# Loading and multiplying the first weight chunks of a decoder layer by rows of blocks

## The reference, cut to what matters

```python
def rms_norm(x, g):
    y = xf * lax.rsqrt(jnp.mean(xf * xf, axis=-1, keepdims=True) + EPS)
    return (y * g.astype(jnp.float32)).astype(x.dtype)

def swiglu(h, w_gate, w_up, w_down):
    return (jax.nn.silu(h @ w_gate) * (h @ w_up)) @ w_down

h = rms_norm(x, ffn1_norm[i])
x = x + 0.5 * swiglu(h, ffn1_w_gate[i], ffn1_w_up[i], ffn1_w_down[i])
```

## Time and profile before

| what | value |
|---|---|
| median of 3 runs | 938.45 us (937.75 to 938.58) |
| profiled execution, its own time | 938.35 us |
| its span, first to last instruction | 936.6 us |
| PE busy | 923.4 us, 99% of the span |
| ACT, POOL, DVE busy | 385.3, 414.0, 297.9 us |

### The profile page before, as it was taken

How to read it: one execution, slowest core, us unless ns; L and a number is a source line. 1 busy time by engine, 2 the same in 40 slices (tenths; PEclk the granted TensorE clock), 3 DMA queues, 4 the chain that set the end, 5 groups by cost and what they waited for, 6 DMA issues and landing times.

```text
span 936.6 us, 11393 instructions
## 1 busy us (share of the span) xinstructions
PE 923.4 (99%) x4104; PEld 759.6 (81%) x4104; DVE 297.9 (32%) x467; ACT 385.3 (41%) x514; POOL 414.0 (44%) x191
## 2 busy tenths in 40 slices
PE   7999999999999999999999999999999999999998
PEld 5888888888888888777788788888888888888886
DVE  6511122211100501659978532111112200410532
ACT  5734444433321421565844644433444321321641
POOL 3554444444444444345645354444444444444340
PEclk9999999999999999999999999999999999999999
DMA  8333333332332333231223143333333323332221
GB/s 251 108 113 99 102 90 94 108 90 90 107 95 90 90 112 90 60 99 34 68 68 113 54 126 103 99 90 94 107 90 91 108 93 90 99 103 90 74 73 56
DMA packets 129650, 89.25 MB, mean 95 GB/s; under 512 B 11312, under 2 KB 114776, under 8 KB 129624
## 3 DMA queue, kind: packets, MB, share of 16 engines
q1 hardware_dynamic: 129608, 88.90, 31.9%
q10 hardware_dynamic: 16, 0.00, 0.0%
HBM read 86.80 MB, written 2.10 MB: 95 GB/s over the span
## 4 chain that ended last, share of the span: by engine, by line
PE 94%; DVE 4%; issue 1%; DMA 0%; ACT 0%; DVEq 0%; ACTq 0%
PE bank L1114 31%; PE bank L1115 31%; PE bank L1116 31%; PE bank L1129 1%; DVE sumsq L745 1%; DVE h_lo L736 1%; DVE probs L923 1%; PE bank L1260 0%; DMA x_nat<-in_x 0%; PE bank L1134 0%; DVE x_t L1088 0%; DVE tmp L1087 0%; DVE pr_lo L949 0%; DVE small L931 0%; ACT h_hi L428 0%
## 5 line engine op out<-in xcount | busy, mean ns | idle before, releaser
L324 POOL TENSOR_TENSOR w_lo<-raw,w_hi 128x1024 fp32r<-128x1024 f32 x161 | 390.2, 2426 | 479.1 <-ACT w_hi L468 240.4
L1114 PE MATMUL bank<-h_hi,w_hi 128*128 128x512 f32 x848 | 335.2, 395 | 0.3 <-DVE h_lo L736 0.3
L1115 PE MATMUL bank<-h_lo,w_hi 128*128 128x512 f32 x848 | 330.7, 390 | 0.0
L1116 PE MATMUL bank<-h_hi,w_lo 128*128 128x512 f32 x848 | 330.6, 390 | 0.0
L1114 PEld LDWEIGHTS bank<-h_hi,w_hi 128*128 128x128 f32 x848 | 159.6, 188 | 36.8 <-issue 2.3
L1115 PEld LDWEIGHTS bank<-h_lo,w_hi 128*128 128x128 f32 x848 | 159.7, 188 | 34.5 <-issue 1.9
L1116 PEld LDWEIGHTS bank<-h_hi,w_lo 128*128 128x128 f32 x848 | 159.6, 188 | 33.2
L419 ACT ACTIVATE w_hi<-raw 128x1024 fp32r<-128x1024 f32 x81 | 85.7, 1060 | 223.3 <-PE bank L1116 218.6
L468 ACT ACTIVATE w_hi<-raw 128x1024 fp32r<-128x1024 f32 x80 | 84.4, 1060 | 190.9 <-PE bank L1116 190.9
L1114 PE MATMUL bank<-act_hi,w_hi 128*128 (+1 forms) x352 | 136.9, 389 | 0.0
L1115 PE MATMUL bank<-act_lo,w_hi 128*128 (+1 forms) x352 | 136.9, 389 | 0.0
(11 more groups left out here) (149 smaller groups left out, 621.5 us busy)
## 6 DMA issues: line engine op xcount, KB each, us to landing
raw<-in_ffn_w_gate SPq DMA_DIRECT2D x44, 512.0 KB, 3.7
raw<-in_ffn_w_up SPq DMA_DIRECT2D x44, 512.0 KB, 3.7
raw<-in_ffn_w_down SPq DMA_DIRECT2D x44, 512.0 KB, 3.7
raw<-in_w_ple_gate SPq DMA_DIRECT2D x8, 512.0 KB, 3.7
raw<-in_w_in SPq DMA_DIRECT2D x6, 512.0 KB, 3.7
x_nat<-in_x SPq DMA_DIRECT2D x4, 512.0 KB, 7.0
raw<-in_w_in SPq DMA_DIRECT2D x8, 256.0 KB, 3.2
raw<-in_w_out SPq DMA_DIRECT2D x4, 512.0 KB, 3.4
```

Of the source, the lines that this page charges most:

```text
L324: pool.tensor_tensor(w_lo[:, slot, :], raw[:, slot, :], f32(w_hi[:, slot, :]), ALU.subtract).then_inc(w_ready, 1)
L1114: nc.tensor.matmul(dst, a_hi, b_hi, start=first, stop=False)
L1115: nc.tensor.matmul(dst, a_hi, b_lo, start=False, stop=False)
L1116: return nc.tensor.matmul(dst, a_lo, b_hi, start=False, stop=last)
```

## The change

x is loaded in five parts instead of four (block 0, block 1, then three parts of two blocks), and behind each part come the rows of the same feature blocks of chunks 0 to 3, as one DMA for each block and matrix (128 rows by 256 columns, which are two slots). ACT rounds the rows of all four slots together (`first_split`), POOL and, for block 0, DVE make `w_lo` of them. PE multiplies all four chunks by feature block 0, then by block 1 and so on (`first_step`), k outermost, into banks 0 to 3; blocks 6 and 7 come last, chunk after chunk. `h_hi` and `h_lo` of the first h are made straight from the transposes in PSUM (banks 4 to 6) and no longer from `x_t`; the copy to `x_t` follows. `w_used` and `w_ready` of chunks 0 to 3 are raised at the end of this stretch.

```diff
+    FIRST = ((0, 1), (1, 2), (2, 4), (4, 6), (6, 8))
...
+            def load_first(s):
+
+                k0, k1 = FIRST[s]
+                for j, w in enumerate((ffn1_w_gate, ffn1_w_up)):
+                    for k in range(k0, k1):
+                        sp.dma_start(raw[:, j:SLOTS:2, k * P:(k + 1) * P],
+                                     w[0, k * P:(k + 1) * P, 0:2 * P].rearrange("p (f c) -> p f c", f=2))\
+                            .then_inc(first_loaded[s], 16)
...
-            for c in range(SLOTS):
-                lo_of(c, c + 1)
+            for s in range(1, len(FIRST)):
+                cols = slice(FIRST[s][0] * P, FIRST[s][1] * P)
...
+                ins = pool.tensor_tensor(w_lo[:, :, cols], raw[:, :, cols], f32(w_hi[:, :, cols]), ALU.subtract)
+                if s < len(FIRST) - 1:
+                    ins.then_inc(first_lo_done, 1)
+                else:
+                    ins.then_inc(w_ready, SLOTS)
...
+            def first_round(d):
+                act.wait_ge(x_turned, d + 1)
+                nc.scalar.activation(h_hi[:, d, :], bank[4 + d % 3][:], ACT.Copy,
+                                     scale=gain[:, d:d + 1]).then_inc(h_hi_done, 1)
...
-            rstd_of(0, 4)
-            act.wait_ge(gain_ready, 3)
+            rstd_of(0, 5)
             ffn_scalar(0, FFN1)
...
+            first_rest(0)
+            dve.wait_ge(first_hi_done, 1)
+            nc.vector.tensor_tensor(w_lo[:, :, 0:P], raw[:, :, 0:P], f32(w_hi[:, :, 0:P]),
+                                    ALU.subtract).then_inc(first_lo_dve, 1)
+            first_copy(0)
...
+            pe.wait_ge(gain1_loaded, 16)
+            turn(bank[7][:, 0:KD], gain_nat[0:KD, :], KD).then_inc(gain_turned, 1)
             turn_x(0)
             turn_x(1)
...
-            for j in range(2, SLOTS):
-                pe.wait_ge(w_ready, j + 1)
-                from_h(bank[j][:], j, 0, HALF)
-                if j == 2:
+            first_ready(KD - 2)
+            first_ready(KD - 1)
+            for j in range(SLOTS):
+                from_h(bank[j][:], j, KD - 2, KD).then_inc(w_used, 1)
+                if j == 0:
                     pe.wait_ge(dve_consts, 4 + PAD)
-                    stat(0, 4)
-                from_h(bank[j][:], j, HALF, KD).then_inc(w_used, 1)
+                    stat(0, 5)
             ffn_tensor(0, FFN1)
```

More of the change, by code:

```diff
@@ L819, in later_gains, with first_rest, first_copy @@
                                       sink_in[:].rearrange("p (g t) -> p g t", g=2)).then_inc(gain_ready, 1)
[L822 to L836, removed]
+            def first_rest(d):
+                dve.wait_ge(h_hi_done, d + 1)
+                nc.vector.scalar_tensor_tensor(h_lo[:, d, :], bank[4 + d % 3][:], gain[:, d:d + 1],
+                                               f32(h_hi[:, d, :]), ALU.mult, ALU.subtract).then_inc(h_ready, 1)
+            def first_copy(d):
+                nc.vector.tensor_copy(x_t[:, d, :], bank[4 + d % 3][:]).then_inc(x_ready, 1)
+            dve.wait_ge(gain_turned, 1)
+            nc.vector.tensor_copy(gain[:, 0:KD], bank[7][:, 0:KD]).then_inc(gain1_ready, 1)
+            dve.wait_ge(gain1_ready, 1)
+            first_rest(0)
[3 more added lines that the diff above has]
+            first_copy(0)
+            first_rest(1)
+            first_copy(1)
+            first_rest(2)
+            first_copy(2)
+            h_add(0, 1)
+            first_rest(3)
+            first_copy(3)
+            h_add(0, 2)
+            first_rest(4)
+            first_copy(4)
+            h_add(0, 3)
+            first_rest(5)
+            first_copy(5)
+            h_add(0, 4)
+            first_rest(6)
+            first_copy(6)
+            h_add(0, 5)
+            first_rest(7)
+            first_copy(7)
+            h_add(0, 6)
+            h_add(0, 7)
             later_gains()
@@ L1198, in turn_x @@
             def turn_x(d):
[L1200 to L1205, removed]
+                for s in range(len(FIRST)):
+                    if d == FIRST[s][0]:
+                        pe.wait_ge(x_loaded[s], 16)
+                if d >= 3:
+                    pe.wait_ge(x_ready, d - 2)
                 for b in range(NB):
[L1207 removed]
+                    ins = turn(bank[4 + d % 3][:, b * P:(b + 1) * P], x_nat[:, b, d * P:(d + 1) * P])
@@ L1210, in _ @@
+            pe.wait_ge(gain1_loaded, 16)
+            turn(bank[7][:, 0:KD], gain_nat[0:KD, :], KD).then_inc(gain_turned, 1)
             turn_x(0)
             turn_x(1)
-            pe.wait_ge(gain1_loaded, 16)
-            turn(bank[7][:, 0:KD], gain_nat[0:KD, :], KD).then_inc(gain_turned, 1)
+            first_step(0)
             turn_x(2)
+            first_step(1)
             turn_x(3)
[L1217 to L1220, removed]
-                        pe.wait_ge(w_ready, j + 1)
[L1222 to L1227, removed]
+            first_step(2)
```

98 lines of the change are left out of this document (66 added, 32 removed).

## The result

The changed kernel takes 943.53 us (median; runs from 939.58 to 943.99), the kernel before on the same chip 938.54 us. The ratio, taken over all runs and not from the two medians (which alone would give 1.0053), is 1.0043, 95% interval 1.0032 to 1.0055: slower, by some 4 to 5 us. The forecast was 939.5, its range ended at 942.0, and the time lies beyond that. (One further run of 2941.64 us stands apart from all others. It counts only as one more value above the median, which is 943.49 without it.)

A forecast was written before the change was run, and what follows sets the result against it. PE, busy 923.4 of 936.6 us, was taken as the bound. Start at 7.3, plus 24.8 to the product with ones, plus 7.57 put chunk 4's boundary 1.15 later: 938.35 plus 1.15 is 939.5 us, range 938.0 to 942.0.

The forecast's parts named there:

- the seam: From the product with ones to chunk 4's w_lo: 7.57 us, PE waits 3.5 us, boundary 1.15 us later than before.
- part 1: Opening of the kernel: transfers, transposes, rounding and h_lo let the first matmul start at 7.3 us, earlier by 3.4 us.
- the landing at 4.2: At the start: block 0 of x and its four chunks' rows, 512 KB together, all in at 4.2 us.
- The second rival: At the start: PE starts late or runs dry, first matmul at 8.5 to 9.5, adding 1.2 to 2.2 us; chance 0.13.
- The upper bound of 8.5: First matmul at 8.5 us if POOL's first piece, 1.29 us, comes before DVE's subtraction for w_lo of block 0.
- The clock: Behind PE's 3.5 us gap before chunk 4: clock falls to 1.2 GHz, costing 1.6 us, 941.1 in all; chance 0.27.
- the first rival: Behind the gap before chunk 4: matmuls run at the lower clock, 1.6 us more, 941.1; chance 0.27.
- The table loads: On ACT around Ln and Exp: three loads of 1.28 us each; one load less would make the sum 938.2.
- The third rival: Before chunk 4: its rounding could come before Ln, so PE goes through without a gap, 935.75 us; chance 0.05.

The follow-up runs named there:

- k4_stat: The kernel before, with only the product with ones moved from the middle of chunk 2 into chunk 3, leaving 18 matmuls behind it: 944.06 us, ratio 1.0055.
- k2_table: The changed kernel with one table set holding both ln and exp loaded ahead of Ln: 941.11 us, ratio 1.0023.
- k1_fill: The changed kernel plus 15 matmuls into a bank nobody reads, where PE stood still before chunk 4: 940.81 us, ratio 1.0024.
- k3_order: The changed kernel with the joint ln and exp table set and ACT rounding chunk 4 ahead of Ln: 936.84 us, ratio 0.9981.
- k7_warm: k6_both plus ten small products of ones with ones where PE waits for x and h at the start: 935.92 us, ratio 0.9976.
- k6_both: The changed kernel with joint table set, chunk 4 rounded ahead of Ln, and first transfers issued by ACT and SP: 937.31 us, ratio 0.9982.

## Why the prediction was wrong

By its own steps:

- **What bounds the kernel, and the seam.** Right, to 0.13 us. The stretch from the first matmul to the end of the product with ones was to take 24.8 us and took 24.93; from there to `w_lo` of chunk 4 7.57 were forecast and 7.45 measured (0.07 of the 7.57 was a wait of Ln for its table load, which the later product has behind it); the gap was to be 3.5 us and is 3.47. That the product with ones moved nearer to chunk 4 was named as the change's new wait, and k4_stat shows that this alone makes it.
- **The start (part 1).** Wrong by 1.26 us. The failed step is the landing at 4.2, with "I cost the new transfers, 16 issues for 4 of the chunks and one more of x, at nothing". The landing was worked out by bytes at 0.32 MB a us, as if the three transfers came in like one of 512 KB. Block 0 of x did land at 3.4 as forecast, and the gate rows at 3.9. The up rows, third in SP's row of issues, landed at 5.72: 1.52 late, of which the steps behind gave back 0.26. Half a microsecond for each issue is some 0.3 of it; the rest is that this transfer took 3.9 us where the two ahead of it took 2.7, with only 171 and 220 GB/s flowing between 3 and 5 us. That the way of issuing causes it is shown by the five profiles with shared issue, where the same rows were in 0.5 to 1.5 us earlier; by what path stays open. What hid the transfers later on (a PE slower than they are) does not hide the first one, on which everything waits. The issues of the kernel before, 0.49 us for 512 KB, would have told the smaller part; I had read the landings and not the issues. The second rival named this case, transfers that land behind their share of the bytes, and held it at 0.13. The upper bound of 8.5 stood there for another reason, POOL beside DVE, which did not come: `h_lo` took 0.75 and `w_lo` 0.61, and POOL's first piece began only at 8.69.
- **The clock.** Held at 0.27 and priced at 1.6. It fell in nine of twelve runs, by their average clock, and in the profiled one cost 2.77 us. The step that failed is the choice "no row here shows a fall, and the gap only just gets there". In k2_table the clock fell behind a gap of 2.2 us too, in six of seven runs. The price was taken from the slow stretch at the start, eight matmuls; here it was thirteen to fourteen. The Trainium skill (TensorE: Matmul & The Clock Gate, Why this matters for your kernels) advises to leave no long gap of PE between bursts of matmuls; k1_fill and k4_stat agree with it, and "by that page alone this would be the forecast" was the better of the two.
- **Together.** 939.5 + 1.26 + 2.77 is 943.5, and with the 0.17 of smaller terms the profiled 943.70. The second rival's late start and the first rival's clock came true together, a case which the text did not price: its range took in the clock's case with a start up to 0.9 later, but at 1.6 for the clock.
- **The table loads.** The loads at Ln and Exp are both in the trace, as the prediction took them to be. The Trainium skill (ScalarE: Activation LUTs, Table sets: the hidden batching unit) says that ln and exp share a set; k2_table shows that this holds once the shared set is loaded by an instruction of its own, and then saves 1.28 us in the seam. The kernel as it stood did not ask for it.
- **The third rival.** Rightly held small for the changed kernel. k3_order shows that it is what the change needs: with the seam mended its earlier start is worth 1.75 us (936.84 for 938.59).

## What to carry to other kernels

Where a small product starts a long chain on other engines (here a sum of squares, two functions, a rounding and a subtraction, 7.5 us), count how much of PE's work stands behind it; an order of loops with k outermost moves work from behind such a product to ahead of it, and an earlier start is then worth nothing until the chain is shortened. An idle gap of PE can cost more than its length: here 3.5 us of standing still cost 2.8 more in slow matmuls in the profiled run, and the clock fell in nine of twelve, and work without any use in its place was the cheaper choice. And when a kernel's first operands land is not read off their bytes alone: cut into small transfers, the last of them came 1.5 us behind its share, and issuing them from two engines brought about 1 us of that back.

## What the runs showed of the hardware that I had not expected

- The clock fell behind gaps of 2.2 and 3.5 us in most executions, and not in all: by the average clock of the runs, nine of twelve of the changed kernel, six of seven of k2_table, none of ten in k1_fill, where the gap was filled. In k4_stat it fell only after four matmuls at full pace.
- The granted clock of a stretch reads 0.53 behind the gap, where it agrees with the pace, and 1.00 at the start, where the matmuls go at 0.43 us all the same. At the start of an execution the pace of the matmuls is the measure. The stretch view of the changed kernel:

```profile
8.50:12.70 4.20, 4.14 (x10) 3.34 (x11) 1.86 (x3) 2.26 (x4) 1.93 (x2) 1.00 1.10 344
```

- Small float32 products of ones, with transposes among them, brought PE to its upper level before its first real product (k7_warm, 0.24 us from its second matmul to its third). In the same kernel four transposes took 0.66 us; in k6_both they took 1.12.
- The first issues of DMAs take SP about 0.5 us each, for 128, 256 and 512 KB alike (0.44 to 0.57); with more transfers under way one took 2 us and more (4.06 for two of x in the kernel before).
- Of the first three small transfers of one queue two took 2.7 us from issue to landing and the third 3.9. With two engines issuing, the first weights were in at 4.25 to 4.77 instead of 5.30 to 5.72, and x's block 1 came later.
